# One ring of slots less for the weight tiles: the remainder overwrites the tile that landed, and tiles are split two ahead

## The chip, the cores and the metric

The kernel runs on one core of a Trainium2 chip. The metric is the device time of one execution in microseconds (us). The engines are named as in the profile: PE is TensorE (PEld its weight loads), ACT is ScalarE, DVE is VectorE, POOL is GpSimd, SP is SyncE, which here only issues DMAs.

## The reference, cut to what matters

Two stacks of transformer layers follow one another on one sequence of 512 positions with 1024 features. The first stack has two layers, each with six modulation vectors from a conditioning vector (`c_act @ w_ada`), three branches (retention, spatial gating, a pooled branch), their gates, a projection, and a feed-forward part. The second has one layer of forgetting attention and one of dilated attention, each with a feed-forward part with a short convolution. Everything is float32.

```
mod = c_act @ w_ada[l] + b_ada[l]
h = rms_norm(x, norm1[l]) * (1.0 + sc1) + sh1
proj = h @ w_in[l]
...
merged = jnp.sum(gates * branch_proj, axis=2)
x = x + gt1 * (merged @ w_out[l])
h2 = rms_norm(x, norm2[l]) * (1.0 + sc2) + sh2
hidden = jnp.square(jax.nn.relu(h2 @ w_ff1[l]))
x = x + gt2 * (hidden @ w_ff2[l])
```

## The kernel before, in words

**Weight tiles.** All large weights come as one stream of 648 tiles of 128 x 1024 float32 (512 KB). A product in float32 is made of three products in the fp32r type: the tile is split into `hi` (its value rounded to fp32r) and `lo` (what is left, `raw - hi`), the activations likewise, and `three` adds hi*hi, hi*lo and lo*hi. A usual tile is 24 matmuls of 512 columns.

**The ring.** There are four slots (`RING`), and each has three buffers: `raw`, where the DMA lands, `hi` and `lo`. A tile goes through four queues, each strictly in order:

- SP issues the DMA into `raw` (L320) when the counter `lo_ready` says that the tile four before has been split: the landing slot is free as soon as DVE has read it.
- ACT splits off `hi` (L888, in `tick`) when the tile has landed and PE is done with the tile four before (`tile_done`).
- DVE makes `lo` (L1223, in its own `tick`) after `hi`, and counts `lo_ready` up.
- PE waits for `lo_ready` and for a free PSUM bank, multiplies, and counts `tile_done` up.

**Where the splits stand.** `tick` is called from the loops of ACT and DVE. In the body for tile T, ACT first calls `tick`, which splits tile T + `AHEAD` with `AHEAD` = 3, then waits for PE to be done with T and drains its bank; DVE splits T + 3 and then does the vector work on T. So the split stands in the queue ahead of the work on T and behind the work on T - 1. In groups of the form `tiles_N` four banks are filled together: ACT calls `tick` for all tiles of the group, waits for the last one, then drains four banks.

**Stages of a layer of the first stack.** `rstd` and `root` belong to the norm: POOL adds squares, PE sums them, ACT takes the root (L948), DVE refines it, PE spreads it (L511), and DVE writes `h` in `norm_to` (L1296 and on). Before the first norm of a layer come 16 short tiles of `w_ada` (below: modulation tiles): 4 matmuls each (L467, L468), and after each four of them ACT copies a row (`ada_row`, L924), PE turns it into columns (`ada_columns`, L476) and DVE adds a bias (`ada_out`, L1268). The other 32 modulation tiles stand one by one between usual tiles (`ada=True`). Further stages that matter below: the norm of the gating branch (`v_mean`, L1448 to L1465), which DVE does between two stages while PE is at the next one; `pool_tile` and the four half-size tiles of `w_pool` that follow it (loop `for g in range(4)`); the gated pairs; and the projection `w_out`.

**Peeled groups.** After a norm, and at `w_out`, PE starts a stage with `first_T`: it waits for three split tiles at once and runs them interleaved over k. ACT and DVE call `tick(0)` early for it, ahead of the root, or ahead of the stage, so that the fourth tile of the group is split too.

```
def tick(s, static=None):
    s = (s + AHEAD) % RING
    ...
    act.wait_ge(landed[s], land[s].next(16))
    act.wait_ge(tile_done, split.next())
    act.activation(hi[:, s], raw[:, s], ACT.Copy).then_inc(hi_ready, 1)
```

Of the kernel before, what the change touches and what calls it, by code (L numbers as in the profile page):

```python
# [8 lines left out]
F32R = mybir.dt.float32r  # L9
# [5 lines left out]
P = 128  # L15
# [9 lines left out]
EPS = 1e-6  # L25
NEG = -1e30
RING = 4
AHEAD = RING - 1
TILE = KT * P

N_ADA = 6 * D // P
# [51 lines left out]
def build(nc, stream, xT, cvec, pos, consts, decay, tables, vec1, ws, bs, vec2, wf, outT):  # L83
    with ExitStack() as ctx:
# [4 lines left out]
            return ctx.enter_context(nc.semaphore(name))  # L89


        raw = sb("raw", [P, RING, TILE])
        hi = sb("hi", [P, RING, TILE], F32R)
        lo = sb("lo", [P, RING, TILE], F32R)
        x = sb("x", [P, KT, S])


# [132 lines left out]
        lo_ready = sem("lo_ready")  # L230
# [80 lines left out]
        @block.sync  # L311
        def _(sp):
            for dst, src in ((cst[:], consts), (x[:], xT), (cs[:, 0], cvec), (tab[:, 0:2048], decay)):
                sp.dma_start(dst, src).then_inc(setup_in, 16)
            freed = Count()
            with repeat(sp, TILES // RING, {freed: RING}) as i:
                for s in range(RING):

                    sp.wait_ge(lo_ready, freed.next())
                    sp.dma_start(raw[:, s], stream[bass.ds(i * RING + s, 1)].rearrange("a p c -> (a p) c")  # L320
                                 ).then_inc(landed[s], 16)
            for n in range(KT):
                sp.wait_ge(out_ready, n + 1)
                sp.dma_start(outT[:, n], act3[:, n]).then_inc(out_done, 16)
            sp.wait_ge(out_done, 16 * KT)
# [548 lines left out]
        def _(act):  # L874
# [28 lines left out]
            def tiles_T(n, drain, uses_st=True, last=False, peel=False, ada=False):  # L903
                def body(i, first=False):
                    for s in range(RING):
                        t = None if not last else TILES - RING * (n // RING - i) + s
                        if s or not first:
                            tick(2 * s if ada else s, t)
                        act.wait_ge(tile_done, done.next())
                        drain(i, s)  # L910
                        if ada:
                            tick(2 * s + 1)
                            done.next()
                    if ada:
                        ada_row()
                if peel:
                    body(0, True)
                    bodies(n // RING - 1, {stf: RING} if uses_st else {}, lambda i: body(i + 1))
                    return
                bodies(n // RING, {**({stf: RING} if uses_st else {}), **(dict(ada_ring) if ada else {})}, body, last)  # L920
# [22 lines left out]
            def root(early=True):  # L943

                if early:
                    tick(0)
                act.wait_ge(summed, sums.next())
                act.activation(stat[:, 8:12], pb[:, 4, 0:4], ACT.Sqrt, bias=epsc, scale=1.0 / D).then_inc(rooted, 1)  # L948

# [27 lines left out]
            with repeat(act, LAYERS, {split: LAYER_TILES, done: LAYER_TILES, stf: 8 + 48 + 8 + 8 + 64,  # L977
                                      sums: 6, means: 1, vecs: 1, of: 8, **{c: LAYER_TILES // RING * 16 for c in land}}) as l:
                act.wait_ge(vec_seen, vecs.next())
                root(early=False)  # L980
                with repeat(act, 4, ring):
                    for s in range(RING):
                        tick(s)
                    done.next(4)
                    ada_row()
                tick(0)

                def drain_to(first, func):
                    def drain(i, s):
                        act.activation(act3[:, at(i * RING + s + first), :], pb[:, s:s + 1], func  # L990
                                       ).then_inc(bank_free, 1)
                    return drain

                def drain_tok(first, func):
                    def drain(i, t):
                        act.activation(act3[:, bass.ds(i + first + 2 * t, 1), :], pb[:, t:t + 1], func  # L996
                                       ).then_inc(bank_free, 1)
                    return drain
                tiles_T(8, drain_to(0, ACT.Copy), uses_st=False, peel=True)
                tiles_N(2, drain_tok(8, ACT.Copy))  # L1000
                for h in range(R_HEADS):
                    for e in range(2):
                        act.wait_ge(o_full, of.next())
                        act.activation(Osq[:, e * S:(e + 1) * S], pb[:, 2 + 2 * (h % 2) + e],
                                       ACT.Square).then_inc(osq_ready, 1)
                    act.wait_ge(summed, sums.next())
                    act.activation(root_r[:, 0:S], pb[:, 6], ACT.Sqrt, bias=epsc, scale=1.0 / R_V).then_inc(rooted, 1)
                tiles_T(8, lambda i, s: to_st(s, func=ACT.Silu), ada=True)
                pairs()
                tiles_N(2, drain_tok(8, ACT.Gelu_apprx_tanh), ada=True)  # L1010
                act.wait_ge(v_mean, means.next())
                act.activation(stat[:, 8:12], stat[:, 12:16], ACT.Sqrt).then_inc(rooted, 1)
                tiles_T(8, drain_to(0, ACT.Gelu_apprx_tanh), uses_st=False, ada=True)

                def drain_p(i, s):
                    act.wait_ge(y_ready, l * 56 + 16)
                    drain_to(0, ACT.Copy)(i, s)
                tiles_T(8, drain_p, uses_st=False, ada=True)
                pairs()
                for g in range(4):  # L1020
                    tick(g)
                    act.wait_ge(tile_done, done.next())
                    for e in range(2):
                        n = 2 * g + e

                        to_st(n % 4, scale=v1[:, V_PS + n:V_PS + n + 1], bias=bpps[:, n:n + 1])
                pairs()
                def gate_by(first):
                    def drain(i, s):
                        m = i * RING + s + first  # L1030
                        to_st(s, scale=mod[:, at(m)])
                    return drain
                tick(0)
                to_x(8, gate_by(16), peel=True)
                root()
                tiles_T(8, lambda i, s: to_st(s), peel=True)
                with repeat(act, 3, {split: 16, done: 16, stf: 16, **{c: 64 for c in land}}):
                    tiles_T(8, gate_by(40))
                    tiles_T(8, lambda i, s: to_st(s))
                to_x(8, gate_by(40))  # L1040
# [4 lines left out]
            def conv_ffn(last=False):  # L1045
                root()
                for j, n in enumerate(SLABS):
                    def body(i, first=False):
                        for s in range(RING):
                            if s or not first:  # L1050
                                tick(s)
                            act.wait_ge(tile_done, done.next())
                            to_st(s)
                            if s % 2:

                                act.wait_ge(conv_done, cv.next())
                                act.activation(A[:, s], A[:, s], ACT.Silu).then_inc(gated, 1)
# [152 lines left out]
        def _(dve):  # L1210
# [24 lines left out]
            def tiles_T(n, work, last=False, peel=False, ada=None):  # L1235
                def body(i, first=False):
                    for s in range(RING):
                        t = None if not last else TILES - RING * (n // RING - i) + s
                        if s or not first:
                            tick(s if ada is None else 2 * s, t)  # L1240
                        if work is None:
                            drained.next()
# [66 lines left out]
            def rstd(early=True):  # L1309

                if early:
                    tick(0)
                newton(pb[:, 4, 0:4], stat[:, 8:12], stat[:, 12:16], stat[:, 4:8], 1.0 / D)
                dve.sem_inc(rs_ready, 1)

# [70 lines left out]
            with repeat(dve, LAYERS, {split: LAYER_TILES, drained: LAYER_BANKS, roots: 7, rp: 8, sc: 16,  # L1386
# [5 lines left out]
                    ada_out(i)  # L1392
                dve.drain()
                tick(0)

                dve.tensor_tensor(bpps[:], v1[:, V_BP:V_BP + 8], v1[:, V_PS:V_PS + 8], ALU.mult)
                geff_of(V_N1, 8)
# [129 lines left out]
                        dve.sem_inc(st_free, 2)  # L1527
                tiles_T(16, last_branch)
                tick(0)
                tiles_T(8, add_to_x, peel=True)  # L1530
                geff_of(V_N2, 32)
                norm(geff, mod[:, 24:32], hH, hL, h_ready)
# [17 lines left out]
            def conv_ffn(layer, last=False):  # L1550
                norm(v2[:, W_FFN + 8 * layer:W_FFN + 8 * layer + 8], None, hH, hL, h_ready)
                first = 0
                for j, n in enumerate(SLABS):
                    def body(i, skip=False):
                        for s in range(RING):
                            if s or not skip:
                                tick(s)
                            dve.wait_ge(bank_free, drained.next())

# [59 lines left out]
            def tiles_split(n, work, peel=False):  # L1619
                def body(i, first=False):  # L1620
                    for s in range(RING):
                        if s or not first:
                            tick(s)
                        drained.next()
                        work(i, s)
# [252 lines left out]
```

## Time and profile before

| | |
|---|---|
| median of 3 runs | 3817.14 us (3815.19 to 3817.17) |
| the profiled execution | 3820.45 us, its span 3818.7 us |
| mean granted TensorE clock | 0.95 |
| PE busy | 3499.3 us, 92% of the span |
| DVE busy, ACT busy | 1952.1 us (51%), 1245.6 us (33%) |
| tiles streamed | 648, 512 KB each |

PE's busy time holds modelled ends of pipelined matmuls: a matmul of 512 columns is shown as 390 ns long, while the next one starts some 227 ns after it. The start times are what to read. A timeline row gives start, duration, engine, line, operation, output and inputs, count, and in brackets the idle time before it with what ended it.

### The profile page before, as it was taken

What the parts mean: (1) busy time and instruction counts of PE and PEld (TensorE: products, weight loads), DVE (VectorE), ACT (ScalarE), POOL (GpSimd) and SP (SyncE); (2) the same over time, 40 slices, a digit from 0 to 9 for tenths busy, and PEclk for the clock granted to TensorE, in tenths of its full rate; (3) what the DMA queues carried; (4) which work ended last, traced back from release to release, by engine and by line L of the source; (5) the groups of instructions that cost most, each with busy time, mean ns of one, the idle gap of its engine ahead of it and who ended that gap; (6) DMA issues with size and microseconds to landing.
All of it is one profiled execution on the core that took longest, in us unless ns stands there. A gap on an engine that the chain in (4) does not pass through costs nothing.

```text
span 3818.7 us, 46596 instructions
## 1 busy us (share of the span) xinstructions
PE 3499.3 (92%) x15412; PEld 2838.9 (74%) x15412; DVE 1952.1 (51%) x2665; ACT 1245.6 (33%) x1643; POOL 160.6 (4%) x201
## 2 busy tenths in 40 slices
PE   4989989999998979989999998998999989889998
PEld 3658778778886747777787886866778867777886
DVE  4263355655444364354745445455656652467555
ACT  3224433323234214333432233225323322243333
POOL 1000000010001000000000002002000001210000
PEclk9989999999998989989999999899999989989999
DMA  5213333323224203333322222210223222102222
GB/s 177 83 45 110 110 127 107 108 83 99 94 99 136 97 15 124 116 105 122 109 99 83 94 98 84 72 61 28 77 94 99 95 82 94 56 28 88 93 94 77
DMA packets 95944, 349.33 MB, mean 91 GB/s; under 512 B 10865, under 2 KB 10865, under 8 KB 95569
## 3 DMA queue, kind: packets, MB, share of 16 engines
q1 hardware_dynamic: 95040, 345.34, 27.3%
q0 software_dynamic: 784, 2.47, 0.2%
q8 instruction: 67, 1.10, 0.1%
q14 instruction: 53, 0.43, 0.0%
HBM read 345.67 MB, written 2.10 MB: 91 GB/s over the span
## 4 chain that ended last, share of the span: by engine, by line
PE 75%; DVE 9%; issue 6%; DVEq 3%; POOLq 3%; ACT 3%; DMA 1%; ACTq 0%; POOL 0%; SPq 0%
PE pb L415 20%; PE pb L416 20%; PE pb L417 20%; POOLq L339 3%; PE pb L491 2%; PE pb L493 2%; PE pb L492 2%; DVEq L1565 1%; PE pb L467 1%; PE pb L468 1%; DVE yL L1275 1%; DMA raw<-stream 1%; PE pb L558 1%; PE pb L829 1%; DVE act L1566 1%
## 5 line engine op out<-in xcount | busy, mean ns | idle before, releaser
L1223 DVE TENSOR_TENSOR lo<-raw,hi 128x1024 fp32r<-128x1024 f32 x648 | 806.9, 1253 | 708.9 <-ACT hi L888 631.6
L415 PE MATMUL pb<-hH,hi 128*128 128x512 f32 x2400 | 960.0, 400 | 37.9 <-DVEq L1307 23.7
L416 PE MATMUL pb<-hL,hi 128*128 128x512 f32 x2400 | 952.9, 397 | 0.0
L417 PE MATMUL pb<-hH,lo 128*128 128x512 f32 x2400 | 950.6, 396 | 0.0
L888 ACT ACTIVATE hi<-raw 128x1024 fp32r<-128x1024 f32 x648 | 677.6, 1053 | 276.0 <-PE pb L493 128.1
L415 PEld LDWEIGHTS pb<-hH,hi 128*128 128x128 f32 x2400 | 462.9, 193 | 139.9 <-issue 25.6
L415 PE MATMUL pb<-yH,hi 128*128 128x512 f32 x1344 | 526.0, 391 | 18.2 <-DVEq L1276 18.2
L416 PEld LDWEIGHTS pb<-hL,hi 128*128 128x128 f32 x2400 | 463.1, 193 | 97.5 <-issue 1.0
L417 PEld LDWEIGHTS pb<-hH,lo 128*128 128x128 f32 x2400 | 461.9, 192 | 98.7
L416 PE MATMUL pb<-yL,hi 128*128 128x512 f32 x1344 | 524.9, 391 | 0.0
L417 PE MATMUL pb<-yH,lo 128*128 128x512 f32 x1344 | 524.6, 390 | 0.0
L901 ACT ACTIVATE st<-pb 128x512 f32<-128x512 f32 x328 | 195.8, 597 | 999.8 <-PE pb L417 999.4
L415 PEld LDWEIGHTS pb<-yH,hi 128*128 128x128 f32 x1344 | 253.4, 189 | 74.1 <-DVEq L1276 21.6
L417 PEld LDWEIGHTS pb<-yH,lo 128*128 128x128 f32 x1344 | 253.5, 189 | 52.9
L416 PEld LDWEIGHTS pb<-yL,hi 128*128 128x128 f32 x1344 | 253.5, 189 | 52.4
L1323 DVE TENSOR_TENSOR x<-x,st 128x512 f32 (+1 forms) x136 | 94.1, 692 | 375.1 <-ACT st L901 375.1
L338 POOL TENSOR_TENSOR act<-act 128x512 f32<-128x512 f32 x70 | 94.0, 1342 | 3212.5 <-ACT act L941 3207.6
L901 ACT ACTIVATE st<-pb,mod 128x512 f32<-128x512 f32 x80 | 55.0, 688 | 289.0 <-PE pb L417 289.0
L491 PE MATMUL pb<-hi,hH 128*128 128x512 f32 x256 | 102.7, 401 | 8.0 <-ACT act L996 4.7
L990 ACT ACTIVATE act<-pb 128x512 f32 (+1 forms) x48 | 28.7, 598 | 235.1 <-PE pb L417 235.0
L493 PE MATMUL pb<-lo,hH 128*128 128x512 f32 x256 | 101.4, 396 | 0.0
L492 PE MATMUL pb<-hi,hL 128*128 128x512 f32 x256 | 101.3, 396 | 0.0
(269 smaller groups left out, 3233.0 us busy)
## 6 DMA issues: line engine op xcount, KB each, us to landing
raw<-stream SPq DMA_DIRECT2D x648, 512.0 KB, 3.3
x<-xT SPq DMA_DIRECT2D x1, 2048.0 KB, 8.3
outT<-act SPq DMA_DIRECT2D x8, 256.0 KB, 2.2
tab<-decay SPq DMA_DIRECT2D x1, 1024.0 KB, 9.8
scr<-ws POOLq DMA_DIRECT2D x2, 256.0 KB, 2.9
scr<-bs POOLq DMA_DIRECT2D x2, 256.0 KB, 3.5
tab<-tables POOLq DMA_DIRECT2D x1, 512.0 KB, 3.7
cst<-consts SPq DMA_DIRECT2D x1, 302.0 KB, 2.9
```

What stands on the lines that cost most here:

```text
L338: pool.tensor_tensor(A[:, 0], A[:, 0], A[:, k], ALU.add)
L339: pool.drain()
L415: pe.matmul(out, whi, ahi, start=first, stop=False)
L416: pe.matmul(out, whi, alo, start=False, stop=False)
L417: return pe.matmul(out, wlo, ahi, start=False, stop=last)
L491: pe.matmul(pb[:, t], aH[:, k, a], hi[:, slot, w], start=k == 0, stop=False)
L492: pe.matmul(pb[:, t], aL[:, k, a], hi[:, slot, w], start=False, stop=False)
L493: ins = pe.matmul(pb[:, t], aH[:, k, a], lo[:, slot, w], start=False, stop=k == KT - 1)
L888: act.activation(hi[:, s], raw[:, s], ACT.Copy).then_inc(hi_ready, 1)
L901: act.activation(st[:, s:s + 1], pb[:, b:b + 1], func, bias=bias, scale=scale).then_inc(bank_free, 1)
L1223: dve.tensor_tensor(lo[:, s], raw[:, s], hi[:, s].bitcast(F32), ALU.subtract).then_inc(lo_ready, 1)
L1323: dve.tensor_tensor(x[:, n], x[:, n], st[:, s:s + 1], ALU.add).then_inc(st_free, 1)
```

## The change

`raw` and `lo` become one buffer: `lo` is only a name for the same memory in another type, and DVE's subtraction reads `raw` and writes its result over it. A landing slot is therefore free only when PE is done with the tile, and SP waits for `tile_done` instead of `lo_ready`. `AHEAD` goes from 3 to 2, so every `tick` of a loop body now splits tile T + 2. To have four tiles split ahead of a peeled group, the early `tick(0)` becomes `tick(0)` and `tick(1)` in every such place on ACT and on DVE, and the first body of the group leaves out two ticks instead of one. What is computed stays the same.

```
-AHEAD = RING - 1
+AHEAD = RING - 2
...
+        with nc.sbuf_tensor("lo", [P, RING, TILE], F32R) as lo:
+            pass
         raw = sb("raw", [P, RING, TILE])
         hi = sb("hi", [P, RING, TILE], F32R)
-        lo = sb("lo", [P, RING, TILE], F32R)
...
-                    sp.wait_ge(lo_ready, freed.next())
+                    sp.wait_ge(tile_done, freed.next())
                     sp.dma_start(raw[:, s], stream[bass.ds(i * RING + s, 1)].rearrange("a p c -> (a p) c")
                                  ).then_inc(landed[s], 16)
...
-                        if s or not first:
+                        if s > 1 or not first:
                             tick(2 * s if ada else s, t)
...
                 if early:
                     tick(0)
+                    tick(1)
...
                 tick(0)
+                tick(1)
                 to_x(8, gate_by(16), peel=True)
...
                 tiles_T(16, last_branch)
                 tick(0)
+                tick(1)
                 tiles_T(8, add_to_x, peel=True)
```

The other edits are of these same two forms, in the remaining loops of ACT and DVE.

## Rows read from the trace of the kernel before

**Rows 1.** The page: busy time, share of the span, instructions.
```profile
PE 3499.3 (92%) x15412; PEld 2838.9 (74%) x15412; DVE 1952.1 (51%) x2665; ACT 1245.6 (33%) x1643; POOL 160.6 (4%) x201
```

**Rows 2.** The waits of PE for a split, whole span: us in total, times, longest.
```profile
PE pb L415 <- DVE lo L1223: 13.8, 5, 9.0
```

**Rows 3.** DMA issues: whole span; then stretches 50.0:51.5 and 51.5:53.0 alone.
```profile
raw<-stream SPq DMA_DIRECT2D x648, 512.0 KB, 3.3
...
raw<-stream SPq DMA_DIRECT2D x1, 512.0 KB, 3.2
...
raw<-stream SPq DMA_DIRECT2D x1, 512.0 KB, 4.5
```

**Rows 4.** The waits of SP, whole span.
```profile
SPq L320 <- DVE lo L1223: 3361.5, 644, 87.4
```

**Rows 5.** Timeline, first layer's 16 modulation tiles (start, us, idle before, releaser).
```profile
46.10 0.77 PE L467 MATMUL pb<-hi,cHL 128*128 128x512 f32 x1
...
49.90 2.08 ACT L888 ACTIVATE hi<-raw 128x1024 fp32r<-128x1024 f32 x2 [0.65 <-PE pb L468]
...
58.25 1.06 ACT L888 ACTIVATE hi<-raw 128x1024 fp32r<-128x1024 f32 x1 [0.24 <-DMA raw<-stream]
59.22 0.57 ACT L924 ACTIVATE v<-pb 2x512 f32<-2x512 f32 x1
...
59.84 1.62 PE L476 MATMUL pb<-cst,v 2*128 2x1 f32 x8 [2.38 <-ACT v L924]
...
61.38 0.80 PE L467 MATMUL pb<-hi,cHL 128*128 128x512 f32 x1
...
77.25 1.23 DVE L1223 TENSOR_TENSOR lo<-raw,hi 128x1024 fp32r<-128x1024 f32 x1 [1.13 <-ACT hi L888]
...
79.05 0.75 DVE L1296 SCALAR_TENSOR_TENSOR st<-x,geff,pb 128x512 f32<-128x512 f32 x1 [0.18 <-issue]
```

**Rows 6.** Timeline at the change from the last gated pair to `w_out`.
```profile
788.25 1.23 DVE L1223 TENSOR_TENSOR lo<-raw,hi 128x1024 fp32r<-128x1024 f32 x1 [1.93 <-ACT hi L888]
...
791.83 0.39 PE L415 MATMUL pb<-halved,hi 128*128 128x512 f32 x1
...
796.13 1.22 DVE L1223 TENSOR_TENSOR lo<-raw,hi 128x1024 fp32r<-128x1024 f32 x1 [0.45 <-issue]
```

**Rows 7.** Windows of 6 us after a wait of 4.03 us for L924 (granted clock third from last).
```profile
464.00:470.00 6.00, 6.00 (x19) 5.08 (x19) 3.80 (x7) 0.89 (x1) 0.00 (x0) 0.52 0.01 3
470.00:476.00 6.00, 6.00 (x28) 4.92 (x28) 5.21 (x14) 4.11 (x5) 0.00 (x0) 1.00 0.00 0
```

**Rows 8.** Timeline in the second layer: norm of the gating branch beside its next stage.
```profile
1641.41 0.39 PE L415 MATMUL pb<-hH,hi 128*128 128x512 f32 x1
...
1643.16 1.22 DVE L1223 TENSOR_TENSOR lo<-raw,hi 128x1024 fp32r<-128x1024 f32 x1
```

**Rows 9.** Timeline, first layer: the splits and tiles around `w_pool`.
```profile
698.69 1.23 DVE L1223 TENSOR_TENSOR lo<-raw,hi 128x1024 fp32r<-128x1024 f32 x1 [0.20 <-ACT hi L888]
...
700.15 0.47 PE L415 MATMUL pb<-halved,hi 128*128 128x512 f32 x1 [1.42 <-DVE lo L1223]
...
702.79 1.22 DVE L1223 TENSOR_TENSOR lo<-raw,hi 128x1024 fp32r<-128x1024 f32 x1 [0.29 <-issue]
...
704.15 0.49 PE L415 MATMUL pb<-hH,hi 128*128 128x512 f32 x1 [1.03 <-DVE lo L1223]
```

**Rows 10.** Timeline of ACT at the end of a `tiles_N` group with modulation tiles.
```profile
426.35 1.06 ACT L888 ACTIVATE hi<-raw 128x1024 fp32r<-128x1024 f32 x1 [4.37 <-PE pb L493]
427.43 1.28 ACT L996 ACT_TABLE_LOAD   x1
```

**Rows 11.** Timeline of ACT at the root ahead of the first convolution stage.
```profile
2692.26 1.04 ACT L888 ACTIVATE hi<-raw 128x1024 fp32r<-128x1024 f32 x1
...
2695.30 0.26 ACT L948 ACTIVATE stat<-pb,cst 128x4 f32<-128x4 f32 x1 [0.70 <-PE pb L504]
```

**Rows 12.** The waits of PE from 2790 to 2800, end of the first convolution slab.
```profile
PE pb L415 <- DVEq L1276: 4.5, 1, 4.5
```

More of the change, by code:

```diff
@@ L27 @@
 RING = 4
-AHEAD = RING - 1
+AHEAD = RING - 2
 TILE = KT * P
@@ L89, in sem @@
             return ctx.enter_context(nc.semaphore(name))
+        with nc.sbuf_tensor("lo", [P, RING, TILE], F32R) as lo:
+            pass
         raw = sb("raw", [P, RING, TILE])
         hi = sb("hi", [P, RING, TILE], F32R)
-        lo = sb("lo", [P, RING, TILE], F32R)
         x = sb("x", [P, KT, S])
@@ L317, in _ @@
                 for s in range(RING):
-                    sp.wait_ge(lo_ready, freed.next())
+                    sp.wait_ge(tile_done, freed.next())
                     sp.dma_start(raw[:, s], stream[bass.ds(i * RING + s, 1)].rearrange("a p c -> (a p) c")
@@ L906, in body @@
                         t = None if not last else TILES - RING * (n // RING - i) + s
-                        if s or not first:
+                        if s > 1 or not first:
                             tick(2 * s if ada else s, t)
@@ L946, in root @@
                     tick(0)
+                    tick(1)
                 act.wait_ge(summed, sums.next())
@@ L986, in _ @@
                 tick(0)
+                tick(1)
                 def drain_to(first, func):
@@ L1033, in _ @@
                 tick(0)
+                tick(1)
                 to_x(8, gate_by(16), peel=True)
@@ L1049, in body @@
                         for s in range(RING):
-                            if s or not first:
+                            if s > 1 or not first:
                                 tick(s)
@@ L1238, in body @@
                         t = None if not last else TILES - RING * (n // RING - i) + s
-                        if s or not first:
+                        if s > 1 or not first:
                             tick(s if ada is None else 2 * s, t)
@@ L1312, in rstd @@
                     tick(0)
+                    tick(1)
                 newton(pb[:, 4, 0:4], stat[:, 8:12], stat[:, 12:16], stat[:, 4:8], 1.0 / D)
@@ L1394, in _ @@
                 tick(0)
+                tick(1)
                 dve.tensor_tensor(bpps[:], v1[:, V_BP:V_BP + 8], v1[:, V_PS:V_PS + 8], ALU.mult)
@@ L1529, in _ @@
                 tick(0)
+                tick(1)
                 tiles_T(8, add_to_x, peel=True)
@@ L1555, in body @@
                         for s in range(RING):
-                            if s or not skip:
+                            if s > 1 or not skip:
                                 tick(s)
@@ L1621, in body @@
                     for s in range(RING):
-                        if s or not first:
+                        if s > 1 or not first:
                             tick(s)
```

## The prediction, made before the changed kernel was run

> **What bounds the kernel now.** I read the page first: PE is busy in 92% of the span [rows 1], so the matmuls carry the time, and only what makes PE stand still, or makes it run at the low clock afterwards, can cost or give anything. Then the waits of PE: for the split (`lo`) it waits 13.8 us in five waits, 9.0 of it in one [rows 2]. So the ring hardly holds PE up today. Then SP: it waits 3361.5 us for `lo`, of a span of 3818.7 [rows 4], which says that landed tiles lie idle for long; the stream has time to spare on average. The change spends this reserve. What matters is where the reserve is used today, and the averages hide that, so I went through the timeline stage by stage with two questions: is DVE (or ACT) held by other work while PE runs through tiles that are already split, and does PE run through tiles faster than a slot can be filled again.
>
> **The steady case costs nothing.** A usual tile is 24 matmuls 0.227 us apart, 5.44 us. With the change the DMA for tile T starts when PE is done with T - 4, three tiles (16.3 us) ahead of its use. It lands after 3.3 us [rows 3], and the split takes 1.06 us on ACT and 1.23 on DVE [rows 5]. ACT calls for it after tile T - 3, two tiles (10.9 us) ahead. 5.6 us fit into both. DVE subtracts as many elements as before, reading and writing in SBUF; I take the in-place form at the same 1.23 us. If it differed by 0.1 us, the steady stages would hide that too. SP issues as many DMAs in the same order, and nothing but them stands behind its wait, up to the outputs. Among usual tiles with a modulation tile between, the room is smaller: the DMA starts 0.93 + 5.44 + 0.93 = 7.3 us ahead of its use, and 0.15 + 3.3 + 1.06 + 1.23 and some 0.3 for hand-overs are 6.0. That is hidden with 1.3 us to spare; with the cover gone it is the third rival below.
>
> **Modulation tiles ahead of a layer: the largest loss.** Sixteen tiles of 4 matmuls each. Before, 3 are split and 4 more lie in `raw` when they begin; with the change 2 and 2. More important, the load of tile 5 now starts only when PE is done with tile 1, and ACT must split tile 5 before it can copy the row for tiles 0 to 3, because both stand in one queue, the split first. So each group of four passes through this chain: two tiles on PE (46.10 to 49.85, 3.8 us, at the low clock [rows 5]), 0.1 to issue, the landing, 0.1, ACT's split up to the row copy 0.97 (58.25 to 59.22), the copy up to the columns 0.62, the columns up to the next tile 1.54 (59.84 to 61.38) [rows 5]. The landing: 3.3 us is the median of the run, but here a second DMA follows within 1.7 us, and the row of such a one shows 4.5 where the one before it took 3.2 [rows 3]. The Trainium skill ("DMA: Bandwidth & Descriptors", section "Anatomy of one DMA") puts a DMA at 2.0 us plus bytes over 436 GB/s, which would be 3.2 us for 512 KB, an estimate by the page; the lone transfer agrees, the crowded one doesn't, and by the page's figure four groups in each of two layers would cost about 10 us less than my sum. I take 4.5. The group is then 3.8 + 0.1 + 4.5 + 0.1 + 0.97 + 0.62 + 1.54 = 11.6 us. PE stands still for about 4 us in it, and a stop of 2.38 us was followed by the low clock here, 0.77 and 0.80 us being shown for first matmuls after it [rows 5], so I take the low clock for all groups. Four groups end at 46.10 + 46.5 = 92.6; about 0.5 us for the bias, two splits of 1.23 instead of one in DVE's queue ahead of the norm, and 0.57 (78.48 to 79.05) give 96.1 for the first write of `h`, against 79.05: 17 us. Lower bound: the full clock (3.8 becomes 1.9, 1.54 becomes 1.0) and 3.2 us for the landing make a group 7.9 us, and `h` starts at 81.3, 2 us late. Between the ends I take 15 a layer, near the upper one, because both rows that decide, the low clock and the crowded landing, are from this very stage. Two layers: **+30** (4 to 34).
>
> **`w_out`: PE waits for its third tile.** `first_T` needs three tiles split. Before, the third is split at 788.25, ahead of DVE's work on the last gated pair, and PE goes on at 791.83 without a stop [rows 6]. With the change the split that stands there is the second tile's. The third's is DVE's early `tick(0)`, behind that work, in the place of the split at 796.13. It ends at 797.35, PE starts 0.2 later, at 797.55: 5.7 us. Behind it PE runs at the low clock: after a stop of 4.03 us the windows show the clock at 0.52 and 19 matmuls in 6 us, then 1.00 [rows 7]; at 0.227 us these 19 take 4.3, so 1.7 us are lost and, by the tile that ran there to 473.0, about 2.1 (7.5 instead of 5.44). Two layers: 2 x 7.8 = **+15.6** (11.4 without the clock).
>
> **Norm of the gating branch.** DVE is in this norm while PE does a usual tile, a modulation tile and then the third tile, which PE starts at 1641.41; the next split begins at 1643.16 [rows 8]. Before, that split is the fourth tile's. With the change it is the third's, so PE waits until 1644.4 + 0.2: 3.2 us. The low clock behind it is likely (2.38 us sufficed, above), 2.1 us. Two layers: 2 x 5.3 = **+10.6** (6.4 to 10.6).
>
> **`w_pool`.** DVE is in `pool_tile` and in the splitting of the outputs, one tile split every 4.1 us (698.69, 702.79), and PE, with tiles of only 2.7 us, is already waiting there: 1.42 and 1.03 us [rows 9]. All splits now come one place later: the one ending at 699.9 is the third tile's, the next the fourth's, and the one after, at 706.9 if the spacing of 4.1 holds, the first gate's. That tile starts at 708.3, not 704.15. Two layers: **+8** (7 to 11, with some low clock that DVE's pace mostly hides).
>
> **Where it gives time.** At the end of a `tiles_N` group with modulation tiles, ACT splits a tile as soon as PE is done (426.35), then loads a table (427.43), then drains [rows 10], while PE waits. That split has waited for PE's last tile but one; the one that replaces it needs a DMA started 5.4 us earlier, which lands 3.8 to 4.9 us later, so it ends 0.5 to 1.5 us sooner. Four such groups: **-4** (-6 to -2). In the first slab of each convolution part DVE is the slower engine, and PE waits 4.5 us at its end [rows 12]; one split of 1.2 us leaves that chain. PE meets a new wait of about 2 us early in the slab, which the 4.5 us cover unless the clock falls. Two slabs: **-2** (-2.4 to +6).
>
> **Roots.** The fourth tile's DMA starts with the end of PE's last tile, some 2.2 us before ACT's split at 2692.26; it lands at 2693.5, its split ends at 2694.6, the table load of 1.28 [rows 10] then ends at 2695.9, and the root, which today starts at 2695.30 [rows 11], is 0.6 us late. At the other seven such places I find the root's input later than that by up to 0.5 us. **+1** (0 to 4).
>
> **Sum.** 30 + 15.6 + 10.6 + 8 - 4 - 2 + 1 = 59. The profiled execution took 3820.45 us and gives 3879; the median of the runs is 3.3 us lower, 3817.1, and gives **3876**. With all lower ends, 4 + 11.4 + 6.4 + 7 - 6 - 2.4 + 0 = 20, it is 3838; with all upper ones, 34 + 15.6 + 10.6 + 11 - 2 + 6 + 4 = 79, 3896.
>
> **Rivals.**
> *The modulation stage is nearly hidden.* Its landings come back at 3.2 us and the clock stays up, so that only the three stalls behind DVE remain: about 20 to 35 us, 3845. For it: 3.2 is the row of a lone DMA. Against: PE's stops there get longer, and the crowded landings are this stage's.
> *Only the reserve is spent.* All splits are still in time, because 5.6 us fit into 10.9; time 3811 to 3817. Against: at the three places above DVE's own rows put the split behind PE's need, and these I trust most.
> *The mixed stages break too.* If landings there take 4.9 us and not 3.3, the 6.0 us become 7.6 against 7.3: 0.3 us at each of 64 usual tiles, 19 us on top, 3895. A second DMA does follow the first after 0.93 us, and crowding is what lengthened it [rows 3]; but it is the first of each pair that is urgent, and the lone or first one shows 3.2.
> *The other side: faster.* Splits that come later leave the ends of stages free. The four `tiles_N` groups at 1.5 us and both slabs at 1.2 give 8.4 us, 3809. It decides only if PE's waits for splits together grow by less than 0.8 us, which the stop at `w_out` alone exceeds seven times.
>
> **Chances.** My forecast, all four losses at about these sizes, 3860 to 3896: 0.66. The nearly hidden stage: 0.17. Mixed stages too: 0.11. Only the reserve: 0.04. Faster: 0.02. A measurement tells 0.2% (7.6 us) from no change. All but the last two are slower by more: slower 0.94, within 0.2% 0.04, faster 0.02. The range takes in the hidden stage down to 3843 and the mixed one up to 3898.
>
> **What would show it.** SP's waits name PE's matmuls, not `lo`. The first layer's norm writes `h` near 96 us and not 79, with PE waiting for L924 four times about 4 us. PE waits for `lo` about 6 us ahead of the first matmul of `w_out`, about 3 us in the stage with L1465, and about 4 us more at `w_pool`, each once a layer; the waits for `lo` grow from 13.8 to some 38 us. The feed-forward stages of the first stack, all usual tiles, keep their length. It would be wrong if the modulation groups keep a period of 8 us, if the landing there is 3.3 us, or if PE waits for `lo` among the usual tiles with modulation tiles between.

## The result, and the profile after

The changed kernel takes 3872.3 us (median of 4 runs, 3864.3 to 3876.4), the kernel before 3817.2 (4 runs, 3815.2 to 3817.7): 1.0143 times as long, 95% interval 1.0125 to 1.0161, so 55 us slower. I had predicted 3876. The profiled execution is the fastest of the changed kernel's, 3864.25 us with a span of 3862.5.

The page of the changed kernel, against [rows 1]: PE has the same work, and ACT now stands idle 335.5 us until a weight tile lands. The last line is from the page of the kernel before, the counterpart of the one above it.

```profile
PE 3500.8 (91%) x15412; PEld 2837.9 (73%) x15412; DVE 1955.3 (51%) x2665; ACT 1255.5 (33%) x1643; POOL 161.7 (4%) x201
...
L889 ACT ACTIVATE hi<-raw 128x1024 fp32r<-128x1024 f32 x648 | 681.5, 1053 | 350.3 <-DMA raw<-stream 335.5
...
L888 ACT ACTIVATE hi<-raw 128x1024 fp32r<-128x1024 f32 x648 | 677.6, 1053 | 276.0 <-PE pb L493 128.1
```

The waits of PE, whole span (us in total, times, longest). The second line answers to [rows 2]: 13.8 us have become 40.9, where I had put 38. The first is the columns of the modulation row; before, it was 42.3 us in the same 24 waits.

```profile
PE pb L477 <- ACT v L925: 61.3, 24, 5.1
...
PE pb L416 <- DVE lo L1227: 40.9, 10, 9.9
```

The waits of SP, against [rows 4]: they name PE's matmuls now, so a slot is filled again when PE is done with it.

```profile
SPq L321 <- PE pb L418: 2945.4, 476, 83.5
```

**First layer's modulation stage**, timeline of ACT, and under it the first column matmul of PE and the first write of `h` on DVE, against [rows 5]. Read the idle time in brackets: in each group of four ACT stands 4.6 to 5.3 us for the first landing and 1.3 to 1.7 for the second, and only then does the row's copy come, although PE starts the group's last matmul at 61.78.

```profile
61.91 1.06 ACT L889 ACTIVATE hi<-raw 128x1024 fp32r<-128x1024 f32 x1 [5.28 <-DMA raw<-stream]
64.71 1.06 ACT L889 ACTIVATE hi<-raw 128x1024 fp32r<-128x1024 f32 x1 [1.74 <-DMA raw<-stream]
65.67 0.57 ACT L925 ACTIVATE v<-pb 2x512 f32<-2x512 f32 x1
66.15 2.15 ACT L889 ACTIVATE hi<-raw 128x1024 fp32r<-128x1024 f32 x2
72.90 1.06 ACT L889 ACTIVATE hi<-raw 128x1024 fp32r<-128x1024 f32 x1 [4.61 <-DMA raw<-stream]
75.23 1.06 ACT L889 ACTIVATE hi<-raw 128x1024 fp32r<-128x1024 f32 x1 [1.27 <-DMA raw<-stream]
76.19 0.57 ACT L925 ACTIVATE v<-pb 2x512 f32<-2x512 f32 x1
...
66.29 1.16 PE L477 MATMUL pb<-cst,v 2*128 2x1 f32 x8 [4.12 <-ACT v L925]
...
93.42 0.75 DVE L1300 SCALAR_TENSOR_TENSOR st<-x,geff,pb 128x512 f32<-128x512 f32 x1 [0.18 <-issue]
```

**At `w_out`**, timelines of DVE and PE, against [rows 6]: the third tile's split is the first half of the pair at 814.77, behind the last product (813.63), and PE stands 5.59 us for it. The two windows of 6 us show the granted clock (third from last) at 0.72 and 0.71, where the kernel before has 1.00 from 785 to 803.

```profile
813.63 0.69 DVE L1531 TENSOR_TENSOR halved<-st,halved 128x512 f32 x1
814.77 2.36 DVE L1227 TENSOR_TENSOR lo<-raw,hi 128x1024 fp32r<-128x1024 f32 x2 [0.45 <-issue]
...
816.23 0.76 PE L416 MATMUL pb<-halved,hi 128*128 128x512 f32 x1 [5.59 <-DVE lo L1227]
...
812.00:818.00 6.00, 1.77 (x4) 1.49 (x5) 4.25 (x6) 1.35 (x2) 0.00 (x0) 0.72 0.21 76
818.00:824.00 6.00, 6.00 (x21) 4.71 (x20) 0.00 (x0) 0.00 (x0) 0.00 (x0) 0.71 0.00 0
```

**At `w_pool`**, timeline of PE, against [rows 9]: the wait is 4.12 us and comes one tile earlier, ahead of the third of the four half-size tiles. The second line is the fourth tile's first matmul, the third that of the gate's first tile.

```profile
715.19 0.47 PE L416 MATMUL pb<-halved,hi 128*128 128x512 f32 x1 [4.12 <-DVE lo L1227]
...
719.61 0.40 PE L416 MATMUL pb<-halved,hi 128*128 128x512 f32 x1
...
723.29 0.49 PE L416 MATMUL pb<-hH,hi 128*128 128x512 f32 x1 [0.78 <-DVE lo L1227]
```

**Where the time went.** The instructions that are not splits are the same in both traces, so the stages can be laid side by side by the starts of the same landmark in each: the root ahead of a layer (ACT), the first write of `h` (DVE; these two bound the modulation stage), the root of the gating norm, the root behind `w_out`, and for the second stack its first and its last root. The table gives what each stage takes longer than in the kernel before, in us, for the first and the second layer, with the time before in the heading. The runs are those of the next section; e9 is a second profile of the changed kernel.

| | modulation (36.0, 35.7) | `h` to gating norm (392.7, 393.9) | gating norm to `w_out`'s root (369.9, 370.4) | second stack (1417.8) |
|---|---|---|---|---|
| changed | +15.7, +14.1 | -4.8, -6.1 | +17.4, +16.3 | -7.7 |
| e9 changed, again | +15.6, +16.8 | -0.3, -3.6 | +17.9, +16.6 | -4.1 |
| e1 lookahead only | 0.0, -1.1 | -4.9, -6.6 | +17.6, +17.0 | -4.0 |
| e2 one ring only | +23.3, +22.0 | +16.2, +15.4 | +19.4, +18.7 | +21.9 |
| e3 `w_out` early | +16.4, +15.1 | -2.5, -3.4 | +9.2, +9.2 | -4.4 |
| e4 filler | +15.2, +17.1 | +0.8, -5.9 | +14.7, +14.8 | -3.9 |
| e5 gating norm early | +14.9, +15.1 | -3.6, -4.2 | +11.1, +8.9 | -4.3 |
| e6 row early | +8.3, +7.5 | -4.1, -5.2 | +17.5, +16.9 | -4.2 |
| e10 row earlier | +9.9, +10.6 | -2.8, -5.5 | +14.2, +15.6 | -7.7 |
| e7 all moves | +7.8, +6.6 | -3.9, -4.2 | +3.2, +0.5 | +1.2 |
| e8 own ring, moves | -1.2, +0.1 | -0.7, -2.1 | +2.4, +1.9 | -7.8 |
| e11 and pool three | -0.8, 0.0 | -1.9, -2.1 | -2.5, -1.6 | -4.4 |

Two stages lose, 29.8 and 33.7 us in the first profile; the feed-forward stages (368.1 us in the first layer, the same in both) lose nothing. The table has one profile a row, and single stages differ between profiles without a cause in the edit: e10 changes nothing behind the modulation stage, and its third column is 3.2 and 0.7 us below the changed kernel's.

### The profile page after: what moved, and what is told of

It reads as the page before. It is cut to its first block, busy times and chain, and to the rows that moved or that the text cites. A ratio compares the mean times of both kernels' runs of the same rounds, so it can differ in the third digit from the quotient of the medians.

```text
span 3862.5 us, 46600 instructions
## 1 busy us (share of the span) xinstructions
PE 3500.8 (91%) x15412; PEld 2837.9 (73%) x15412; DVE 1955.3 (51%) x2665; ACT 1255.5 (33%) x1643; POOL 161.7 (4%) x201
## 4 chain that ended last, share of the span: by engine, by line
PE 79%; DVE 7%; issue 5%; ACT 2%; POOLq 2%; DMA 2%; DVEq 2%; POOL 1%; ACTq 0%; SPq 0%
PE pb L416 22%; PE pb L418 22%; PE pb L417 22%; PE pb L492 2%; PE pb L494 2%; PE pb L493 2%; POOLq L340 1%; DMA raw<-stream 1%; PE pb L468 1%; PE pb L469 1%; PE pb L477 1%; PE pb L830 1%; PE pb L559 1%; DVEq L1289 1%; DVE tab L1677 1%
## 5 line engine op out<-in xcount | busy, mean ns | idle before, releaser
L889 ACT ACTIVATE hi<-raw 128x1024 fp32r<-128x1024 f32 x648 | 681.5, 1053 | 350.3 <-DMA raw<-stream 335.5
L416 PE MATMUL pb<-halved,hi 128*128 128x512 f32 x192 | 79.6, 414 | 26.8 <-DVE lo L1227 19.4
```

What stands on the lines that cost most here:

```text
L416: pe.matmul(out, whi, ahi, start=first, stop=False)
```

## Experiments

Theory A: the loss has two separate causes. With two tiles split ahead, three places have DVE busy with other work when PE wants its third tile. With slots freed by PE, the modulation stage waits for landings. The rivals are the one or the other alone. All diffs are against the changed kernel unless it says otherwise.

**e1: the shorter lookahead alone.** The remainders have their ring back, and SP waits for the split again.

```diff
-        with nc.sbuf_tensor("lo", [P, RING, TILE], F32R) as lo:
-            pass
         raw = sb("raw", [P, RING, TILE])
         hi = sb("hi", [P, RING, TILE], F32R)
+        lo = sb("lo", [P, RING, TILE], F32R)
...
-                    sp.wait_ge(tile_done, freed.next())
+                    sp.wait_ge(lo_ready, freed.next())
```

> The kernel before with the lookahead of two and the moved ticks of the change, but with a ring of its own for the remainders and slots freed when the remainder is written. Theory A (two mechanisms: the split order stalls PE where DVE has other work ahead of the third tile, at the gated pool's tiles, at w_out and at the norm of the gating branch; the refill after PE slows the modulation stage): the stalls at w_out (8.3 a layer), at the gating norm (4.8 and 5.8) and at the pool's tiles (2.7) stay, the modulation stage stays within 3 us a layer of before: 3817 + 16.6 + 10.6 + 5.4 - up to 9 (matrix groups, retention) = 3840 to 3850. Rival B (the whole loss comes from the late refill): 3810 to 3820. Rival C (the whole loss comes from the shorter lookahead, in the modulation stage too): 3865 to 3875.

Measured 3836.0 us (5 runs), 1.0047 times the kernel before (1.0033 to 1.0061). In the profile the first modulation stage takes 36.04 us, where it took 36.03 before, and PE stops ahead of `w_out` exactly as in the changed kernel, as its timeline shows:

```profile
800.68 0.77 PE L415 MATMUL pb<-halved,hi 128*128 128x512 f32 x1 [5.59 <-DVE lo L1226]
```

So the whole loss between gating norm and `w_out` (+17.6, +17.0) comes with the lookahead alone, and none of the modulation stage's does. The time is 4 us below my range, since `h` to gating norm gave back 11.5 where I had allowed up to 9, and the second stack 4.0.

**e2: the one ring alone.** The edits to the ring and to SP's wait as in the change, but three tiles split ahead and the ticks where they were.

```diff
 RING = 4
-AHEAD = RING - 2
+AHEAD = RING - 1
```

> The kernel before with the remainders written over their landing slots and slots freed by PE, but three tiles split ahead as before. Theory A: the stalls at w_out, gating norm and pool tiles go away; the modulation stage gets longer still than in the changed kernel, since the row's copy stands behind the split of a tile that can't land until 3 us and more after the fourth last tile is done, one tile later than with two ahead: + 18 to 24 us a layer instead of 15.7; the groups with the tile's columns on the moving side lose some 4 us each at their drains. Together 3865 to 3890. Rival B (late refill alone is what costs, all places): as the changed kernel, 3872. Rival C (lookahead alone): 3815 to 3825.

Measured 3961.0 us (5 runs), 1.0376 (1.0362 to 1.039). Every expectation was too low by 70 us and more. The modulation stage did what I had worked out (+23.3, +22.0), and the stops that theory A ascribes to the lookahead went: with the same matmuls of both traces laid side by side, PE loses 0.0 us at the gating norm and at `w_pool` in either layer, and 0.9 and 0.8 at `w_out`. The loss in the table's third column lies between these places. What I had missed shows in ACT's waits, whole span:

```profile
ACT hi L889 <- DMA raw<-stream: 1395.6, 527, 12.0
```

527 of 648 splits are waited for on ACT, against 129 in the changed kernel. With three ahead, ACT asks for the next tile as soon as it has drained a bank, and that tile's transfer began only when PE ended the very tile that was drained; the next drain stands behind this in ACT's queue. ACT's timeline in a mixed stage:

```profile
603.63 1.06 ACT L889 ACTIVATE hi<-raw 128x1024 fp32r<-128x1024 f32 x1 [2.64 <-DMA raw<-stream]
605.76 1.06 ACT L889 ACTIVATE hi<-raw 128x1024 fp32r<-128x1024 f32 x1 [1.07 <-DMA raw<-stream]
606.73 0.58 ACT L991 ACTIVATE act<-pb 128x512 f32 x1
610.37 1.06 ACT L889 ACTIVATE hi<-raw 128x1024 fp32r<-128x1024 f32 x1 [3.06 <-DMA raw<-stream]
```

So the two halves of the change do not add up: the lookahead alone costs 19 us, the ring alone 144, both together 55. Given one ring, two ahead is much better than three. How much of the 144 comes by way of late drains, and how much by late splits alone, no run separates.

**e3: third tile of `w_out` split early.** On ACT the same in `pairs`.

```diff
-                tiles_T(16, last_branch)
-                tick(0)
+                tiles_T(12, last_branch)
+                for s in range(RING):
+                    tick(s)
+                    if s == 3:
+                        tick(0)
+                    dve.wait_ge(bank_free, drained.next())
+                    last_branch(3, s)
                 tick(1)
```

> The changed kernel with one split moved: the third tile of w_out is split on ACT and DVE ahead of the last gated pair's product instead of behind it. Theory A (the 5.6 us wait of PE at w_out is DVE being busy with the last product): PE's wait there falls under 1 us in both layers and with it the low clock behind it; the time falls by 13 to 17 us to 3856 to 3859 (ratio to the kernel before 1.010 to 1.011). Rival (the tile lands late, so that the wait is the transfer's): the wait stays, no change within 2 us.

Measured 3860.8 us (4 runs), 1.0111 (1.0095 to 1.0127), 11.5 below the changed kernel and a little less than expected, with executions from 3852 to 3867. In the profile the stage is 8.2 and 7.0 us shorter, 15.3 together. PE's wait, timeline:

```profile
814.04 0.47 PE L416 MATMUL pb<-halved,hi 128*128 128x512 f32 x1 [0.44 <-DVE lo L1233]
```

The wait was DVE's order and not the landing.

**e4: matmuls to fill PE's wait.**

```diff
                 half_k.next(8)
+                for _ in range(20):
+                    pe.matmul(pb[:, 4], hH[:, 0, 0:P], hH[:, 1], start=True, stop=True)
                 tiles_T(8, halfB, halfM, (half_ready, m0), peel=True)
```

> The changed kernel with 20 extra matmuls of 128 by 512 into an unused bank on PE just ahead of w_out's first four tiles, where PE waits 5.6 us for a split (their result is thrown away). Theory A says that the low clock behind the wait costs about 2.1 us a layer on top of it: with PE kept busy the granted clock stays at 1.00 and the time falls by 3 to 5 us. Rival (the loss of 8.3 us a layer there is all waiting, for the split and for the refill that comes late after it): 0, or up to 1 us slower a layer if the extra matmuls outlast the wait.

Measured 3870.6 us (4 runs), 1.0138 (1.0122 to 1.0153): not to be told from the changed kernel, where I had expected 3 to 5 us less. The profile can tell. Timeline and window of PE: the extra matmuls cover the wait up to 1.07 us, and the clock behind it is 1.00, not 0.71.

```profile
815.28 4.70 PE L625 MATMUL pb<-hH 128*128 128x512 f32 x20
821.05 0.47 PE L416 MATMUL pb<-halved,hi 128*128 128x512 f32 x1 [1.07 <-DVE lo L1229]
...
818.00:824.00 6.00, 4.93 (x22) 3.78 (x21) 3.43 (x4) 1.06 (x1) 0.00 (x0) 1.00 0.03 12
```

From this first matmul to PE's first sum for the norm behind `w_out` it is 47.96 us here (869.01 - 821.05), 50.38 in the changed kernel (866.61 - 816.23), 47.84 before (839.67 - 791.83): the low clock costs 2.5 us. In the second layer the same distances are 47.94, 49.45 and 47.84: 1.6.

**e5: third tile behind the gating branch's groups split early**, ahead of the norm, on both engines (the following `tiles_T` is peeled and leaves its first tick out).

```diff
                 tiles_N(2, ada=6)
+                tick(0)
...
-                tiles_T(8, None, ada=8)
+                tiles_T(8, None, peel=True, ada=8)
```

> The changed kernel with one split moved: the third tile after the gating branch's matrix groups is split on ACT and DVE ahead of the branch's norm instead of behind it. Theory A (PE waits there for DVE, which is busy with the norm): the 4.8 and 5.8 us lost there in the two layers fall under 1 us, the time falls by 9 to 11 us to 3861 to 3863. Rival (the tile's landing is late there): PE's wait stays and the norm starts later by it: no change or 1 to 3 us slower.

Measured 3862.5 us (4 runs), 1.0125 (1.0109 to 1.014), 9.8 below the changed kernel by the medians and 7 by the ratios, whose intervals overlap; it is the profile that decides. The waits of PE for `lo` in that stage, 2.4 and 3.3 us in the changed kernel's two layers, are gone; the stage is 6.4 and 7.4 us shorter. In the changed kernel they read, from 465 to 500 and from 1655 to 1710:

```profile
PE pb L416 <- DVE lo L1227: 2.4, 1, 2.4
...
PE pb L416 <- DVE lo L1227: 3.3, 1, 3.3
```

**e6 and e10: the row's copy ahead of the last split, or of the last two** (`s == 1` in e10), on DVE the same with `ada_out`.

```diff
                     for s in range(RING):
                         tick(s)
-                    done.next(4)
-                    ada_row()
+                        if s == 2:
+                            ada_row()
```

> The changed kernel with the row's copy (ACT) and the columns' sum (DVE) of each group of four modulation tiles put ahead of the group's last split instead of behind it. Theory A (the stage's period of 10.5 to 11.6 us is a loop of landing, split, PE and the row's copy, and the row stands behind a split that waits for a tile landing): the period falls to 9 to 10 us, the two stages by 5 to 9 us each, the time to 3855 to 3862. Rival (the loop is landing, two splits and PE alone, since a tile's transfer starts only when PE is done with the tile four back, whatever the row does): 0 to 2 us a stage.

> As the run with the row's copy ahead of the group's last split (3856), but with it ahead of the last two splits. That run's period was 8.4 to 9.6 us, where landings were waited for on ACT ahead of most splits. If the loop of landing, split and PE is what is left, the row can't gain more, and a row that is waited for by PE ahead of the last two splits holds those up: 0 to 4 us a layer slower than that run, 3856 to 3864. Rival (the row is still late and its place is all that matters): 2 to 3 us a layer faster, 3850 to 3852.

Measured 3856.2 us (4 runs), 1.0103 (1.0087 to 1.0118), and 3856.8 (4 runs), 1.0114 (1.0099 to 1.0129). The stage is 7.4 and 6.6 us shorter in e6 than in the changed kernel; in e10 it is 1.6 and 3.1 us longer than in e6, as expected of a row that is no longer late. ACT's timeline of e6 shows what is left: groups of 9.4 us (60.82 to 70.22), and nearly every split waited for its landing.

```profile
60.82 0.59 ACT L925 ACTIVATE v<-pb 2x512 f32<-2x512 f32 x1 [2.04 <-PE pb L469]
61.31 1.04 ACT L889 ACTIVATE hi<-raw 128x1024 fp32r<-128x1024 f32 x1
64.04 1.06 ACT L889 ACTIVATE hi<-raw 128x1024 fp32r<-128x1024 f32 x1 [1.69 <-DMA raw<-stream]
65.50 1.06 ACT L889 ACTIVATE hi<-raw 128x1024 fp32r<-128x1024 f32 x1 [0.40 <-DMA raw<-stream]
68.16 1.06 ACT L889 ACTIVATE hi<-raw 128x1024 fp32r<-128x1024 f32 x1 [1.60 <-DMA raw<-stream]
70.22 0.59 ACT L925 ACTIVATE v<-pb 2x512 f32<-2x512 f32 x1 [1.01 <-PE pb L469]
```

Half of the stage's loss was the row standing behind a late split; the other half, some 8 us a layer, stays. That it is the loop from PE's end of a tile over landing and split to PE fits these waits and is not shown further: no run took it away with one ring.

**e7: all moves**, with one more: the third of `w_pool`'s tiles split early, as in e3.

> The changed kernel with all of the moves at once: early splits at w_out, at the gating norm and at the gated pool's tiles, and the modulation stage's row ahead of the last split. If the losses are local and add up: 3872 - 16.6 - 10.5 - 5.4 - 10 to 18 = 3821 to 3830, still above the kernel before by what the late refill costs in the modulation stages. Rival (each removed stall comes back further on): over 3840.

Measured 3830.1 us (5 runs), 1.0037 (1.0024 to 1.0051). They add up, to 42 us of the 55. One did next to nothing: it took PE's wait of 4.12 us for the third tile of `w_pool` away, and PE waits 4.36 us there for the fourth, whose split stands on DVE behind two outputs' halves. Timelines of DVE and PE:

```profile
702.98 0.69 DVE L1290 TENSOR_TENSOR yL<-st,yH 128x512 fp32r<-128x512 f32 x1
703.96 1.22 DVE L1237 TENSOR_TENSOR lo<-raw,hi 128x1024 fp32r<-128x1024 f32 x1 [0.29 <-issue]
...
705.43 0.76 PE L416 MATMUL pb<-halved,hi 128*128 128x512 f32 x1 [4.36 <-DVE lo L1237]
```

**e8: e1 with the three early splits** (`w_out`, gating norm, `w_pool`), and **e11: the same with `w_pool`'s splits all one tile earlier**, on ACT and on DVE.

```diff
                 for g in range(4):
-                    if g:
-                        tick(g)
+                    if g < 3:
+                        tick(g + 1)
```

> The kernel with the lookahead of two but a ring of its own for the remainders (the first run of this study, 3836) and the three early splits (w_out, gating norm, pool's tiles); the modulation stage is as in the kernel before. If what that run lost are those three places and what it gained at the drains of the matrix groups stays: 3836 - 16.6 - 9.6 - 6 = 3804, range 3800 to 3810, faster than both kernels. Rival (the moved splits only bring the lookahead of three back at these places, gains at the drains go too): 3815 to 3819.

> The own-ring kernel with the three early splits (3810.4), and in the gated pool's tiles all splits one tile earlier, as with a lookahead of three. There PE still waited 4.4 us for the fourth tile's split, behind the preparation of the pool's halves on DVE. Theory: the 2.5 us a layer lost there go: 3804 to 3807. Rival (the wait moves to the next split behind it): 3809 to 3812.

Measured 3810.4 us (11 runs), 0.9987 (0.9978 to 0.9996), and 3802.8 us (5 runs), 0.9963 (0.995 to 0.9977). e8 came out just above my range, with the `w_pool` wait still there. In e11 the waits there are 1.4 and 1.0 us in each layer, as in the kernel before, and it is faster than both kernels, by 13 us than the kernel before. Its ring of remainders stays, so it gains by the order of the splits alone.

**e9: the changed kernel again.**

> The changed kernel once more, unaltered, for a second profile. The first had a span of 3862.5 at a mean granted clock of 0.950 where its other executions ran at 0.946 to 0.948 and took 3868 to 3875. If the spread is the clock's and not a wait's: the landmarks of the stages with waits (modulation + 15.7 and + 14, gating norm + 4.8 to 5.8, w_out + 8.3) repeat within 0.5 us each, and what differs by more lies in stretches where PE has the same instructions and waits and only the granted clock differs (retention, the narrow matmuls of the gate before the attention). If waits differ: PE's idle time for splits differs by 5 us or more.

Measured 3872.3 us (4 runs), 1.0148 (1.0132 to 1.0163), the profiled one with a span of 3877.7, 15.2 us longer than the first profile's of the same program. PE's waits are the same (40.8 us for `lo`, 60.4 for the row, against 40.9 and 61.3). I had expected the stages with waits to repeat within 0.5 us. The first layer's three did; of the second layer's, the modulation stage is 2.7 us longer, with no more waiting for the row (16.2 us against 16.7), the gating norm costs 1.0 us less and `w_out` 0.9 more. What differs beyond that stands in stretches with equal instructions. Windows of the first profile: 80 us from the first rotation of the second layer's retention, then 2 x 6 us from the first narrow matmul (32 columns) of the second stack; the granted clock is third from last.

```profile
1386.44:1466.44 80.00, 57.30 (x161) 31.18 (x160) 55.14 (x72) 13.76 (x18) 0.00 (x0) 0.87 0.03 8
2491.60:2497.60 6.00, 6.00 (x55) 5.96 (x54) 0.69 (x1) 0.60 (x1) 0.00 (x0) 0.98 0.27 89
2497.60:2503.60 6.00, 6.00 (x21) 5.23 (x22) 1.02 (x9) 2.40 (x4) 0.00 (x0) 0.50 0.00 0
```

The same of the second profile:

```profile
1394.44:1474.44 80.00, 58.99 (x148) 31.57 (x148) 50.79 (x66) 11.39 (x16) 0.00 (x0) 0.80 0.01 2
2503.30:2509.30 6.00, 6.00 (x41) 6.00 (x39) 0.69 (x1) 0.60 (x1) 0.00 (x0) 0.70 0.29 89
2509.30:2515.30 6.00, 6.00 (x28) 5.90 (x29) 0.42 (x5) 0.00 (x0) 0.00 (x0) 0.50 0.00 0
```

161 matmuls fall into the 80 us against 148. The narrow matmuls take 8.5 us in the one (2491.6 to 2500.1) and 11.5 in the other (2503.3 to 2514.8), where all but the first 2.4 us is at the low clock. The kernel before takes 11.4 us for them (2440.2 to 2451.6), also at the low clock from 2.4 us on; so 3 us of what the first profile shows as a gain in the second stack are luck. The 8 us by which the first profile lies below its median are probably of this kind, but the executions at the median have no profile.

## Why the prediction was right

**Steady tiles: right.** The feed-forward stage of the first layer kept its 368.1 us, and the mixed stages showed no wait for `lo` but the one behind the gating norm; the in-place split takes 1.25 us, as before. e2 shows that the mixed stages can break: with one ring and three ahead the stages between `h` and the gating norm lose 15 to 16 us a layer.

**Modulation, +30: right in mechanism, and in size with some luck.** 29.8 and 32.4 us in the two profiles. The chain gave groups of 11.6 us; columns lie at 54.69, 66.29, 76.81 and 88.10, groups of 11.6, 10.5 and 11.3. It gave 17 us a layer, and the 15 that I wrote down was a choice below it. Its deciding term was the crowded landing of 4.5 us rather than 3.3: the first transfer of each group landed after 3.1 to 3.2 us, and the second, which is the one on the chain, after 5.1, 4.2, 4.0 and 4.3; all others of the stage took 4.4 to 5.7. By the Trainium skill ("DMA: Bandwidth & Descriptors", section "Anatomy of one DMA"), whose fit the page gives for DMAs issued by GpSimd, one of 512 KB takes 3.2 us, an estimate by which I would have been some 10 us lower; these transfers, issued by SP, agree where one is alone and don't where they overlap. e1 (0.0, -1.1) shows that the one ring makes the loss, and e6 that the row's place makes half of it.

**`w_out`, +15.6: right.** 5.6 us of wait twice, and 2.5 and 1.6 of low clock behind (e4). With the same matmuls of both traces laid side by side, PE falls back by 8.3 and 7.4 us there, 15.7. e3 took 15.3 of it back. The Trainium skill ("TensorE: Matmul & The Clock Gate", section "HAM oscillation — how this bites in real kernels") says that a wait of PE for a DMA lets its clock fall, so that the next tile starts slow; the windows agree for a wait for a split, 0.71 behind the stop and 1.00 where e4 fills it.

**Gating norm, +10.6: right.** On both sides of the norm PE lost 4.8 and 5.8 us, 10.6 in all, 2.4 and 3.3 of it in waits; the granted clock behind the first stop is 0.83 and 0.89 in the windows from 483 to 495, and no run here filled this stop to price it. e5 took 13.7 back in the profile and 9.8 in the medians; what it took back beyond the loss is no bigger than what single stages differ by.

**`w_pool`, +8: right.** I had put the third tile's start at the place of the split ending at 699.9 and the gate's first tile at 708.3 instead of 704.15, 4.15 us later. Measured from the same point (PE comes to `w_pool` 15.06 us later than before), the third tile starts at 700.13 and the gate's at 708.23, 4.1 us late; of these PE gets 0.5 back within two tiles. So the place costs 3.6 us in either layer, 7.1 in all. In the changed kernel PE waits for the third tile's split; e7 shows that the fourth's stands right behind it, and only e11, which moves them all, removes the loss, though with a ring of its own.

**Gains, -4 - 2 + 1: right where I had put them, and too small in all.** At the ends of the four matrix groups PE's stop for the row was 4.03 us each and is 3.07 to 3.36, 3.3 us in all (3.04 each in e1). In the convolution slabs PE has a new stop of 2.5 us for `lo` early on, and the one at the end falls from 4.5 to 1.5; the two convolution parts together are 1.5 us shorter. The root ahead of the first one is 0.6 us late, as put: the matmuls before it run 46.45 us behind the kernel before, the root 47.04. Timeline of PE in the changed kernel, one such stop of each kind:

```profile
473.21 0.98 PE L477 MATMUL pb<-cst,v 2*128 2x1 f32 x4 [3.07 <-ACT v L925]
...
2775.10 0.49 PE L416 MATMUL pb<-hH,hi 128*128 128x512 f32 x1 [2.54 <-DVE lo L1227]
...
2846.94 0.50 PE L416 MATMUL pb<-yH,hi 128*128 128x512 f32 x1 [1.51 <-DVEq L1280]
```

But `h` to gating norm gave back 10.9 us in the first profile and 3.9 in the second, the second stack 7.7 and 4.1. Of the second stack, 1.7 us come from the part with its second attention, which I had not counted. Much of the remainder is the granted clock, in which the two profiles differ and for which I had no term.

In sum: the two lossy stages cost 63.5 us in the first profile (29.8 + 33.7; place by place the latter is 15.7 + 10.6 + 7.1) and 67 in the second, where my four terms gave 64. All else gave back 20 and 8, where I had 5. So the first profile ends 43.8 us behind the kernel before and the second 59.0; the medians lie 55 apart, and my sum was 59.

**Rivals.** A nearly hidden modulation stage would have needed a group of 8 us. Mixed stages that break too did so in e2, not in the change. Neither the reserve alone nor a gain was ever near, though e11 shows that two ahead need not cost anything with a ring of its own.

## What to carry to other kernels

Ask of a lookahead not whether a load fits into it on average, but at each change of stage which split stands behind which other work in the queue of the engine that makes it: three such places cost about 33 us here, and issuing one split ahead of that work gave nearly all of it back at two of them, and at the third it took four, tried only with a ring of its own. Overwriting a landing slot moves its release from the splitter to the last reader; then a longer lookahead is worse than a shorter one, because, as e2's waits show, the splitter's queue stops on landings and what stands behind (drains, row copies) stops with it. Two ways of saving buffers or distance may be priced apart, but must be run together: here 19 and 144 made 55.

## What the runs showed of the hardware that was not expected

Two profiles of one program, with PE's waits equal within 1 us, differed by 15.2 us in span, at mean granted clocks of 0.950 and 0.945. The differences sit in a few stretches: retention (0.87 against 0.80 over 80 us) and the narrow matmuls, where the granted level fell from 2.4 to 1.2 GHz after 6 us in one and after 2.4 in the other, though PE was busy in 6.00 of 6.00 us and had come from full tiles without a pause. Behind equal stops of 1.28 us for a modulation row it is the same: the windows behind the one at 494.50 in the kernel before show 1.00, those around its counterpart at 508.80 in the changed kernel 0.82 and 0.90, and that tile takes 1.6 us longer. The Trainium skill ("TensorE: Matmul & The Clock Gate", section "Part 1: The HAM clock gate") says that at its start the same kernel shows different counts of matmuls at the low clock from run to run, and puts that ramp under 1% of a typical span. Here the counts differ from run to run too, and in the middle of the kernel; the two spans differ by 0.4%, more than a quarter of the effect under study. With such a spread the stage table of one profile is sharper than the medians, but only for stages whose granted clock is compared as well.
